# Retention heads: the first head's order of sums, values and mixing, and the last head's mixing ahead of both gate products

## The reference, cut to what matters

```
q, k, v, g = split(h @ w_in);  q = rope(q);  k = rope(k) * dk**-0.5
scores = (q @ k.T) * decay            # causal by chunks of 64, decay**distance
o = scores @ v                        # per head, 512 positions x 512
o = (o - mean(o)) * rsqrt(var(o) + EPS) * gn_g
y = silu(g) * o
h = h + y @ w_out
```

## Time and profile before

| | us |
|---|---|
| median of 3 runs | 1876.36 (1873.23 to 1876.77) |
| the profiled execution | 1875.02 |
| its span, first to last instruction | 1873.2 |
| PE busy in the span | 1829.0 (98%) |
| the four heads' retention stage, from h11 of the first head to the last head's transposes | 558 to 922 of the span |

### The profile page before, as it was taken

The page is one execution under the profiler, slowest core; times in us unless marked ns, Lnnn a source line. Parts: engine busy times, 40 slices in busy tenths (PEclk is TensorE's granted clock), DMA queues, the critical chain, the costliest instruction groups (busy, mean ns, idle before and its releaser), DMA issues.

```text
span 1873.2 us, 23918 instructions
## 1 busy us (share of the span) xinstructions
PE 1829.0 (98%) x9348; PEld 1554.8 (83%) x9348; DVE 1164.6 (62%) x1863; ACT 883.0 (47%) x1366; POOL 1021.7 (55%) x447
## 2 busy tenths in 40 slices
PE   9999999999997999999899999999999999999998
PEld 7778889898885788888789898998888887888886
DVE  6987775775685645353575445457777767454546
ACT  5345343343463535353545445355666646443444
POOL 5673466474446565655538566665223336674755
PEclk9999999999998999999999999999999999999999
DMA  5222414423258656564352241403333322424221
GB/s 186 90 90 68 158 56 155 139 96 118 71 155 215 199 118 222 112 225 103 99 175 101 85 136 49 155 23 94 97 110 112 102 85 84 147 68 135 90 90 57
DMA packets 150704, 218.61 MB, mean 117 GB/s; under 512 B 4512, under 2 KB 94896, under 8 KB 150080
## 3 DMA queue, kind: packets, MB, share of 16 engines
q1 hardware_dynamic: 134880, 187.97, 30.0%
q0 software_dynamic: 8448, 16.78, 5.2%
q10 hardware_dynamic: 7264, 12.34, 2.3%
HBM read 207.59 MB, written 9.48 MB: 116 GB/s over the span
## 4 chain that ended last, share of the span: by engine, by line
PE 73%; DVE 10%; POOL 4%; ACT 4%; issue 2%; DMA 2%; ACTq 0%; DVEq 0%
PE ps L884 24%; PE ps L885 23%; PE ps L886 23%; POOL w_lo L850 4%; ACT w_hi L1451 1%; DVE ps L2408 1%; DMA raw<-in_ret_w_in_dram 1%; DMA work<-in_ret_w_in_dram 1%; DVE diagonals L2076 1%; DVE probs_t_lo L2882 0%; PE ps L1228 0%; DVE xl L2102 0%; DVE work L2876 0%; ACT work L1956 0%; PE ps L1325 0%
## 5 line engine op out<-in xcount | busy, mean ns | idle before, releaser
L850 POOL TENSOR_TENSOR w_lo<-raw,w_hi 128x1024 fp32r<-128x1024 f32 x220 | 533.4, 2436 | 591.4 <-ACT w_hi L1451 591.4
L884 PE MATMUL ps<-xh,w_hi 128*128 128x512 f32 x1280 | 504.8, 394 | 4.2 <-DVE xl L2102 2.0
L886 PE MATMUL ps<-xh,w_lo 128*128 128x512 f32 x1280 | 499.2, 390 | 0.0
L885 PE MATMUL ps<-xl,w_hi 128*128 128x512 f32 x1280 | 498.8, 390 | 0.0
L1451 ACT ACTIVATE w_hi<-raw 128x1024 fp32r<-128x1024 f32 x238 | 247.6, 1057 | 378.4 <-PE ps L886 333.0
L884 PEld LDWEIGHTS ps<-xh,w_hi 128*128 128x128 f32 x1280 | 240.6, 188 | 59.0 <-issue 8.6
L885 PEld LDWEIGHTS ps<-xl,w_hi 128*128 128x128 f32 x1280 | 240.7, 188 | 50.7 <-issue 1.9
L886 PEld LDWEIGHTS ps<-xh,w_lo 128*128 128x128 f32 x1280 | 240.5, 188 | 50.5
L884 PE MATMUL ps<-hid,w_hi 128*128 128x256 f32 (+1 forms) x688 | 229.0, 333 | 2.5 <-DVE att_v L2836 0.9
L885 PE MATMUL ps<-hid,w_hi 128*128 128x256 f32 (+1 forms) x688 | 227.5, 331 | 0.0
L886 PE MATMUL ps<-hid,w_lo 128*128 128x256 f32 (+1 forms) x688 | 227.3, 330 | 0.0
(11 more groups left out here) (294 smaller groups left out, 3458.6 us busy)
## 6 DMA issues: line engine op xcount, KB each, us to landing
raw<-in_mlp_w_dram SPq DMA_DIRECT2D x40, 1024.0 KB, 5.4
work<-in_mlp_w_dram SPq DMA_DIRECT2D x16, 1024.0 KB, 5.8
raw<-in_ret_w_in_dram SPq DMA_DIRECT2D x12, 1024.0 KB, 6.4
raw<-in_att_w_in_dram SPq DMA_DIRECT2D x12, 1024.0 KB, 5.3
raw<-in_w_gate_dram SPq DMA_DIRECT2D x11, 1024.0 KB, 5.3
raw<-in_w_up_dram SPq DMA_DIRECT2D x11, 1024.0 KB, 5.3
raw<-in_w_in_dram SPq DMA_DIRECT2D x9, 1024.0 KB, 5.1
down<-in_mlp_w_dram SPq DMA_DIRECT2D x8, 1024.0 KB, 5.7
```

Of the source, the lines that this page charges most:

```text
L850: nc.gpsimd.tensor_tensor(half_of(wl[:, b % 2, :], b, half), half_of(source, b, half), half_of(wh[:, b % 2, :], b, half).bitcast(F32), ALU ...
L884: nc.tensor.matmul(o, a[0], b[0], start=first, stop=False, skip_group_check=True)
L885: nc.tensor.matmul(o, a[0], b[1], start=False, stop=False, skip_group_check=True)
L886: return nc.tensor.matmul(o, a[1], b[0], start=False, stop=last, skip_group_check=True)
```

## The change

For the first head (h = 0):
- PE multiplies d2 and d3 with the sums where they were made (`sum_operand`, `sum_ready`), not with copies that were brought back. The scores wait for the last sum only from the third tile on. All four tiles are mixed ahead of d4, and `head_mix` waits for each value tile by itself.
- SP no longer brings back d2 and d3 for it. It fetches the next head's q weights behind the conversion of h11, stores d2, then waits for `p3_landed` and stores d3, waits for `p4_landed`, fetches k and o0, and stores d1 last.
- ACT converts h22's weights ahead of `scale_far(0)` and `position_sum_hi("d3")`. d4's weights are converted behind the copies of mixed tiles 0 and 1, the next q's behind tile 2, and square root and gate follow tile 3. The value tiles wait until both halves of a quarter have been taken.
- DVE makes h22's low sum ahead of the two gate sums, and k's low part behind `keep_product(2)`. The root comes ahead of the gate copies.

For the last head all tiles are mixed ahead of h21 and d4, each transposed tile has its own wait (`last_turn`), and tiles 0 to 2 are gated in one instruction each. Heads 1 and 2 keep their order, with a wait for each value tile in `head_mix`. Head 1 waits for the sums' semaphore for d1, and head 2's d1 is the first one brought back.

```diff
-                            for kind in ("d1", "d2", "h22", "d3"):
-                                n = SUM_ROW[kind]
-                                sp.wait_ge(sum_lo, n + 1)
-                                if kind != "h22":
-                                    sp.dma_start(sums_dram[n], sum_made_in[n].bitcast(F32).rearrange("p n a c -> p n (a c)")).then_inc(sum_stored[n], 16)
-                                else:
-                                    sp.wait_ge(sum_stored[SUM_ROW["d2"]], 16)
-                                    fetch_sum("d2")
+                            converted("h11", 0)
+                            fetch("q", 1)
+                            store_sum("d2")
+                            sp.wait_ge(p3_landed, 16)
+                            store_sum("d3")
+                            converted("d3", 0)
+                            sp.wait_ge(p4_landed, 16)
+                            fetch("k", 1)
+                            fetch("o0", 0)
+                            store_sum("d1")
...
-                        pe.wait_ge(sum_lo, len(SUM_ROW))
                         for j in range(ST):
+                            if j == 2:
+                                pe.wait_ge(sum_lo, len(SUM_ROW))
...
-                        if more:
+                        if h and more:
                             head_quarter("d4", h)
                         pe.wait_ge(pt_ready, c.next(pt_ready, 4))
-                        head_mix(h, (0, 1))
+                        head_mix(h)
                         if not more:
                             head_quarter("h21", h)
-                        head_mix(h, (2, 3))
-                        if not more:
+                        if not h or not more:
                             head_quarter("d4", h)
...
+                        else:
+                            last_turn()
...
+                    def last_turn():
+
+                        pe.wait_ge(o_copied, c.next(o_copied, 2))
+                        for i in range(ST):
+                            pe.wait_ge(p_ready, c.next(p_ready))
+                            for j in range(4):
+                                mm = nc.tensor.transpose(ps[:, 4 + j, P * i:P * (i + 1)],
+                                                         o_sb[:, i, P * j:P * (j + 1)], ident[:, :])
...
                     position_sum_hi("h22")
+                    after_unit()
+                    after_unit()
                     act.wait_ge(sum_lo, SUM_ROW["d2"] + 1)
                     scale_far(0)
                     position_sum_hi("d3")
```

More of the change, by code:

```diff
@@ L1190, in head_quarter @@
                                     sum_ready(kind, h)
[L1191 removed]
+                                mm = product(ps[:, bank, :], head_operand(kind, h, k, slice(P * half, P * (half + 1))), [t[:, k, :] for t in w],
                                              kind in ("h11", "d1", "h21") and k == 0, kind in ("h22", "h21", "d4") and k == 3)
@@ L1743, in gate_curve, with scale_gate @@
                         nc.scalar.activation(sg[:, s, :], sg[:, s, :], ACT.Silu, scale=rc[:, s:s + 1]).then_inc(gate_made, c.made(gate_made))
-                    def scale_gate(h):
+                    def scale_gate(h, tiles=range(ST)):
                         act.wait_ge(root_refined, h + 2)
-                        for s in range(ST):
+                        for s in tiles:
                             act.wait_ge(gate_made, 4 * h + s + 1)
@@ L2716, in head @@
                         value_lo(1)
-                        if more and h:
+                        if h and more:
                             gate_sum(h, 0)
@@ L2723, in head @@
                         value_lo(3)
-                        if more:
+                        if h and more:
                             gate_copy(0)
                             gate_copy(1)
-                            if h == 0:
-                                scale_x(range(0, 2))
                             mixed_stats()
@@ L2732, in head @@
                                 gated(i)
-                        else:
+                        elif more:
+                            scale_x(range(0, 2))
+                            mixed_stats()
+                            refine_root(root_guess)
+                            gate_copy(0)
+                            gated(0)
+                            gated(1)
+                            gate_copy(1)
+                            gated(2)
+                            gated(3)
+                        else:
+                            mixed_stats()
+                            refine_root(root_guess)
+                            normalised(3)
                             gate_sum(h, 0)
                             gate_sum(h, 1)
-                            mixed_stats()
+                            gated(0)
+                            gated(1)
                             gate_copy(0)
-                            refine_root(root_guess)
-                            normalised()
                             gate_copy(1)
-                            for i in range(ST):
-                                multiplied(i)
+                            gated(2)
+                            multiplied(3)
                         dve.wait_ge(p_ready, c.now(p_ready))
```

174 lines of the change are left out of this document (101 added, 73 removed).

## The result

| | before | after |
|---|---|---|
| median of 4 runs | 1876.57 us (1873.23 to 1877.89) | 1863.07 us (1862.68 to 1863.35) |
| the profiled execution | 1875.02 | 1863.28 |
| its span | 1873.2 | 1861.3 |

The ratio is 0.9931, with a 95% interval of 0.9913 to 0.9948: the change makes the kernel faster, by 13.5 us as medians and 11.9 us as spans. The forecast was 1857.9, with a range of 1853.5 to 1866.5. The time lies in the range, 5.2 us above the forecast. In the spans, where the sum was made, 18.5 us were promised and 11.9 came. The medians of the kernel before in the four sets of runs told of here were 1875.40, 1876.23, 1876.57 and 1876.81, and the changed kernel was run in one set only, so a distance from 1863.07 of under some 1.5 us says little.

A forecast was written before the change was run, and what follows sets the result against it. PE was busy 98% of the span, so only its gaps could give time: 15.9 us in the first head plus 2.6 in the last, 18.5 off 1875.0, plus 1.3 to the median, gave 1857.9; range 1853.5 to 1866.5.

The forecast's parts named there:

- h22: First head: h22's weights converted earlier, so its 7.74 us idle shrinks to a stall of 0.2 to 1.3, taken as 0.9.
- The rule on shut-out instructions: At h22: DVE's two-SBUF-input low parts could hold POOL up whole, stall some 1 us longer; 1.1 per pair used instead.
- d3: First head: add p3 issued at 577.3 and landing in 8.5 to 10.5 us cuts d3's 4.08 stall to 1.0.
- The rival of slow adds: First head: p3 still takes 14.4 us, 7.3 lost at d3 instead of 1.0, time 1864.2; chance 0.13.
- Mixing ahead of d4: First head: 0.7 stall before mixed tile 2 where 2.51 stood, and 0.3 at d4 where 0.56 stood.
- The clock in the first head: First head: slow matmuls behind the gaps at h22 and d3 vanish, 1.45 us each.
- The last head: Last head: mixing all tiles first and gating earlier makes outputs start 2.1 earlier; gain taken as 2.6 with the clock.
- outputs at 919.4, 5.1 after d4's end: Last head: copy, gate curve, multiplication and four transposes after d4's end at 914.3 let outputs start 2.1 us earlier.
- tiles 0 and 1 are gated before d4 ends, and eight transposes run at once: Last head: statistics done during h21 and d4, so only the last tiles' gating and transposes remain after d4.
- The term for the clock: Last head: if the clock holds through short pauses, 0.8 of 1.1 us saved, otherwise none; 0.5 counted.
- my own case: Whole kernel: the main forecast holds, time 1854 to 1861 us; chance 0.67.
- the last head gains nothing: Last head: chain from d4 over gate, scaling and multiplication on alternating engines stays as long, time 1860.5; chance 0.13.

The follow-up runs named there:

- experiment 11: Changed kernel with the next q weights' fetch and the store of sum d1 issued where POOL issues p3: 1867.10 us, 4.0 above the changed kernel.
- experiment 3: Changed kernel, POOL alone waiting for all gated tiles before making the output weights' low halves in the last head: 1860.32 us, 2.75 below the changed kernel.
- experiment 4: Changed kernel, ACT converting the last head's first output weights behind all four gate curves: 1858.42 us, 4.65 below the changed kernel.
- experiment 2: Kernel before with only the change's new last head: 1878.92 us, ratio 1.0017, 2.7 above the kernel before in the same set.
- experiment 1: Changed kernel with its last head put back to the old order, first head still changed: 1859.37 us, ratio 0.9916, 3.7 below the changed kernel.
- experiment 7: experiment 4 with the first half of the output weights converted earlier, in ACT's pause behind the scaled gates of tiles 0 and 1: 1858.57 us.
- experiment 8: experiment 7 plus 2, 1 and 6 matmuls without use behind tiles 1, 2 and 3 in PE's pauses: 1854.72 us, ratio to before 0.9881.
- experiment 9: Kernel before with only h22's early weight conversions on ACT: 1872.81 us, 2.6 below the 1875.40 of before in the same set.

## Why the prediction was right in range and 5 us short

- **h22.** Forecast: starts at once, 0.9 of stall from POOL's second half. Measured 0.79. Right. The rule on shut-out instructions was set aside there for the row of 5.76, and POOL's pair took 5.26, inside the bounds of 4.69 and 5.76. How much of that is DVE's doing is not shown: a pair that stands right behind the issue of an add takes 5.25 where no DVE instruction with two SBUF inputs runs beside it too (586.14 before, 588.33 in the changed kernel). But the rule bears on both sides, and DVE's low part of k, which I looked at for POOL's sake alone, took 4.67. That is the 0.30 at h22's second bank.
- **d2.** Costed at nothing, 0.38 measured. ACT's hi part of the sum d3 came at 580.39, so the conversion behind it started at 581.31, where I had only asked when p2 lands.
- **d3.** Forecast 1.0, measured 0.75, with p3 at 9.3 inside 8.5 to 10.5. The rival of slow adds fell: experiment 11 shows that two neighbours of its size make p3 that slow.
- **Mixing ahead of d4.** 0.7 and 0.3 forecast, 0.93 and none measured.
- **The clock in the first head.** Both slow stretches went, as forecast.
- So the first head has 3.15 in pauses against the 2.9 forecast, and with small losses at half boundaries 14.9 gained of 15.9.
- **The last head is the step that failed**: +2.6 forecast, −3.0 measured, 5.6 of the 6.6 us that the spans lack (the other 1.0 is the first head's). Its first term, 0.9 for mixing first, was right (1.0). The term "outputs at 919.4, 5.1 after d4's end" was 8.56 from the start of d4's last matmul, some 3.3 more. What failed is its premise, "tiles 0 and 1 are gated before d4 ends, and eight transposes run at once": the pair was gated from 898.09 to 901.70, and four transposes ran. The prediction did not ask what stands ahead of the gating. One thing was POOL's low halves of the output weights, at 895.96 to 901.15, which DVE's pair outlasted by 0.55: experiment 3 takes them away, and the outputs start 2.2 us sooner, with 0.7 less lost to slow matmuls. The other was ACT's conversion of these weights between the gate curves, which made the pair start late: experiment 4 takes that away too and reaches 5.40. The Trainium skill (SBUF — State Buffer, "SBUF: two separate sides") says just this of a VectorE instruction with two SBUF inputs beside a GpSimd one that reads SBUF; the trace agrees, with 3.61 against 1.41. The prediction used the rule for h22 and not here.
- The term for the clock, 0.5 saved, was −1.8. I had allowed that the clock holds through the short pauses, or else that nothing changes, and no end on the side of loss. The traces show one. Pauses of 1.67 and 2.36 left 8 slow transposes and 15 slow output matmuls in the changed kernel, and 8 and 11 in experiment 2; the one wait of 4.66 left 16 slow transposes and 3 slow output matmuls in experiment 1, and 16 and 5 before. Transposes and outputs together, the low clock cost 3.9 and 3.0 us with the short pauses and 2.4 and 2.9 with the long one. So short pauses spared nothing here, and part of the slowness moved from the transposes to the outputs.
- **Luck.** The time lies outside my own case (1854 to 1861). It falls inside the range because the range had room for the slow adds (1864.2), and they did not come. That rival is the nearest by number, and its mechanism did not happen. The rival "the last head gains nothing" (1860.5) had the right place and too mild a price. It said that the chain behind d4 is as long as before, which the trace showed, but for another reason than its own: the shut-out and ACT's order, not the count of instructions on alternating engines, as experiment 4 shows.
- The profiled execution of before lies 1.5 below its median and the one of after at its median. So 13.5 us came as medians where the spans have 11.9, and these 1.6 us are chance too.

## What to carry to other kernels

Before you move work of VectorE to a new place, lay GpSimd's timeline beside that place. A VectorE instruction with two inputs in SBUF took 1.5 to 3.9 times its length beside GpSimd's pairs here, and the low parts ended about as late as if they had begun when the pair ended. So price such an instruction at the end of GpSimd's pair plus its own length, and move GpSimd's work away where VectorE's is nearer the end of the chain. Price what PE's pauses do to the matmuls behind them, with an end on the side of loss, since two short pauses cost as much here as one long one. Matmuls without use, counted by their measured time, can fill them. Test the parts of such an edit alone and by undoing them: the same conversion was worth 2.6 us alone and 6.2 in company. And before you give a gain to an edit, look where in the two traces it lies: of 3.85 us between experiments 7 and 8, 1.6 lay behind the edit.

## What the runs showed of the hardware

- Two engines working on different data in SBUF lengthen each other's instructions a great deal. VectorE's low part of k takes 1.21 with GpSimd idle, and 3.10 or 4.67 beside its pair; h22's low sum takes 1.22, and 1.90 or 3.79; the gating pair takes 1.41 or 3.61. The four low parts beside a pair all ended 1.08 to 1.09 us behind it, and the gating pair 0.55 behind. VectorE instructions with one input in SBUF kept their 0.69 to 0.70. GpSimd's pair loses less: 5.19 beside the gating pair, where it takes 4.70 in experiment 3.
- A DMA of 1 MB that adds to what it lands on took 8.1 to 14.8 us in all. At one place, p3, it took 9.1 to 9.5 in the ten kernels with nothing of its size issued beside it, and 13.8 to 14.6 in the four with two such transfers (the kernel before, experiments 2, 9 and 11). So its neighbours set its length, and one of 14.8 stands in the changed kernel too, at 622.65.
- PE's granted clock fell to half in or behind every wait of 3 us and more that is told of here. It fell as well in the second of two pauses of 1.67 and 2.36 with four transposes between them, and after pauses of 0.57, 0.29 and 1.96 (experiment 4) and of 0.57, 0.29 and 1.40 (experiment 7). It stayed at 1.00 when matmuls without use stood in them. The price is not fixed: the waits of 7.74, 4.08, 3.73 and 3.66 are followed by seven slow matmuls each, that of 3.14 by eight, that of 6.90 by eleven and that of 5.26 by thirteen, and the wait of 2.51 ahead of the mixing by none in the kernel before and by ten in experiment 9. What decides that stays open.
- Filling was not tried in the first head, where all pauses are now under 1 us and at full clock, and nothing in the trace asks for it.
